# HGRN outputs built token by token on four column tiles, inside the projection's matmuls

## The reference

```python
proj = h @ w_in                                   # q_x, f_x, i_x, g_x, each 8 heads x 128
f = lb + (1.0 - lb) * sigmoid(f_x);  q = silu(q_x);  k = 1.0 - f;  v = i_x
b = cumsum(log(f)) within each chunk of 32
q_rel, k_rel = q * exp(b - b_ref), k * exp(b_ref - b)
a = where(causal, q_rel @ k_rel.T, 0);            o_intra = a @ v
q_dec, k_dec = q * exp(b), k * exp(b_last - b)
# per chunk: o_inter = q_dec @ state;  state = exp(b_last) * state + k_dec.T @ v
o = rms_norm(o_intra + o_inter, o_norm) * silu(g_x)
return o @ w_o
```

## Time and profile before

| | |
|---|---|
| median of 3 runs | 1761.29 us |
| the profiled execution | 1760.62 us, span 1758.8 us, granted clock 0.973 |
| PE busy | 1640.3 us (93%) |
| DVE, ACT, POOL busy | 843.3, 750.8, 649.2 us |
| HGRN heads, loop turns 2 to 7 | some 1129 to 1314 us of the span |

### The profile page before, as it was taken

The page is one execution under the profiler, slowest core; times in us unless marked ns, Lnnn a source line. Parts: engine busy times, 40 slices in busy tenths (PEclk is TensorE's granted clock), DMA queues, the critical chain, the costliest instruction groups (busy, mean ns, idle before and its releaser), DMA issues.

```text
span 1758.8 us, 28713 instructions
## 1 busy us (share of the span) xinstructions
PE 1640.3 (93%) x10394; PEld 1343.9 (76%) x10394; DVE 843.3 (48%) x1461; ACT 750.8 (43%) x1160; POOL 649.2 (37%) x376
## 2 busy tenths in 40 slices
PE   5999979988888999999999999899999999999996
PEld 4787668856566778878888888788878878888885
DVE  6556768856775635522121235566663632111125
ACT  2333334443744445524141347667674622222231
POOL 4453320004421125634444444223334544444441
PEclk9999999989899999999999999899999999999997
DMA  8632210003111112233333331122223233333331
GB/s 288 204 85 72 72 38 3 4 18 87 53 48 34 50 56 78 84 88 92 97 94 97 94 108 48 48 72 72 72 60 92 56 93 96 96 95 95 96 97 59
DMA packets 250958, 140.33 MB, mean 80 GB/s; under 512 B 10121, under 2 KB 242656, under 8 KB 250864
## 3 DMA queue, kind: packets, MB, share of 16 engines
q1 hardware_dynamic: 249552, 137.12, 26.6%
q0 software_dynamic: 1008, 1.66, 0.4%
q10 hardware_dynamic: 304, 0.26, 0.0%
HBM read 136.93 MB, written 2.10 MB: 79 GB/s over the span
## 4 chain that ended last, share of the span: by engine, by line
issue 40%; PE 24%; POOL 11%; DVE 11%; ACT 5%; DVEq 4%; DMA 2%; ACTq 1%; POOLq 1%; SPq 1%
PE bank L750 13%; POOL w_low L555 10%; DVE hg_state L2065 2%; PE bank L1039 2%; DVE bank L2062 2%; PE bank L801 2%; DVEq L2492 1%; DMA x_tok<-in_x 1%; DVE hg_k_dec L2062 1%; PE bank L1199 1%; PE bank L1200 1%; DVEq L2805 1%; PE bank L1227 1%; SPq L439 1%; ACTq L2011 1%
## 5 line engine op out<-in xcount | busy, mean ns | idle before, releaser
L555 POOL TENSOR_TENSOR w_low<-w_raw,w_high 128x1024 fp32r<-128x1024 f32 (+2 forms) x218 | 517.2, 2373 | 964.3 <-ACT w_high L1489 964.2
L750 PE MATMUL bank<-act_high,w_high 128*128 128x512 f32 x976 | 392.4, 402 | 12.1 <-POOL w_low L555 8.4
L750 PE MATMUL bank<-act_high,w_low 128*128 128x512 f32 x976 | 382.7, 392 | 0.0
L750 PE MATMUL bank<-act_low,w_high 128*128 128x512 f32 x976 | 382.6, 392 | 0.0
L1489 ACT ACTIVATE w_high<-w_raw 128x1024 fp32r<-128x1024 f32 (+2 forms) x218 | 219.1, 1006 | 282.2 <-PE bank L750 269.7
L750 PEld LDWEIGHTS bank<-act_high,w_high 128*128 128x128 f32 x976 | 184.4, 189 | 65.3 <-issue 12.3
L750 PEld LDWEIGHTS bank<-act_high,w_low 128*128 128x128 f32 x976 | 184.2, 189 | 40.3
L750 PEld LDWEIGHTS bank<-act_low,w_high 128*128 128x128 f32 x976 | 184.5, 189 | 38.9 <-issue 2.4
L750 PE MATMUL bank<-hid_high,w_high 128*128 128x512 f32 x472 | 184.9, 392 | 3.8 <-DVE mix_out L2734 3.8
L750 PE MATMUL bank<-hid_low,w_high 128*128 128x512 f32 x472 | 184.4, 391 | 0.0
L750 PE MATMUL bank<-hid_high,w_low 128*128 128x512 f32 x472 | 184.3, 390 | 0.0
(11 more groups left out here) (570 smaller groups left out, 2860.0 us busy)
## 6 DMA issues: line engine op xcount, KB each, us to landing
w_raw<-in_mlp_w SPq DMA_DIRECT2D x128, 512.0 KB, 4.0
w_raw<-in_hgrn_w_in SPq DMA_DIRECT2D x32, 512.0 KB, 4.0
w_raw<-in_w_in SPq DMA_DIRECT2D x29, 512.0 KB, 4.0
w_ada_piece<-in_w_ada SPq DMA_DIRECT2D x5, 2048.0 KB, 16.0
w_raw<-in_w_out SPq DMA_DIRECT2D x8, 512.0 KB, 3.8
w_raw<-in_mla_w_o SPq DMA_DIRECT2D x8, 512.0 KB, 3.8
w_raw<-in_hgrn_w_o SPq DMA_DIRECT2D x8, 512.0 KB, 3.8
w_raw<-in_mla_w_in SPq DMA_DIRECT2D x6, 512.0 KB, 4.0
```

The lines of the kernel that those rows point to most:

```text
L555: gp.tensor_tensor(WL[:, c0 % 2, 0:kt, 0:m], WR[:, c0 % 2, 0:kt, 0:m], WH[:, c0 % 2, 0:kt, 0:m].bitcast(F32), ALU.subtract).then_inc(w_lo, 1)
L750: mm = pe.matmul(bank[0:m, :], w[:, k, 0:m], a[:, k0 + k, :], start=(k == 0 and n_ == 0), stop=(k == kt - 1 and n_ == 2))
```

## The change

The outputs become token-major: 32 tokens of the masked scores, or of `hg_q_dec`, are the stationary operand (128x32), the values or the state move (128 columns), and the four chunks of a token tile go to four column tiles of the array. In the loop they are issued inside job 2, after its third slice of K. The root mean square is then a sum along the free axis on VectorE (`tensor_reduce`), the normalisation a multiply from PSUM into a new tile `hg_out_tok`, and four transposes on TensorE bring the result back to feature-major before the last multiply. f is formed by `scalar_tensor_tensor` with the offset broadcast as third operand, and in the loop after the fourth state; k is formed after the states; `low_of_output` goes ahead of job 0's scaling. On ScalarE the gate's SiLU and the squares stand ahead of q's SiLU, the copy of the outputs goes, and a set that holds Ln and Exp is loaded ahead of the exponentials. Some semaphores of the first block are merged (`v_sd` into `u_ready`, `kk_sq` and `rk_ready` into `sums_ready`).

```diff
@@ tensor, hgrn
-                if o is not None:
+                def outputs():
                     for t in range(TT):
-                        pe.matmul(PB[6][:, t * P:(t + 1) * P], VG[:, t, :], AT[:, t, :], start=True, stop=False)
+                        for b in range(P // HC):
+                            pe.matmul(PB[6][b * HC:(b + 1) * HC, t * P:(t + 1) * P], AT[:, t, b * HC:(b + 1) * HC],
+                                      VG[:, t, :], start=True, stop=(t + b == 0))
                         for b in range(P // HC):
                             c_ = t * (P // HC) + b
                             if c_:
                                 pe.wait_ge(g_st, o * (NC - 1) + c_)
-                                mm = pe.matmul(PB[6][:, c_ * HC:(c_ + 1) * HC], ST[:, c_, :],
-                                               QDEC[:, c_ * HC:(c_ + 1) * HC], start=False,
-                                               stop=(b == P // HC - 1))
+                                mm = pe.matmul(PB[6][b * HC:(b + 1) * HC, t * P:(t + 1) * P],
+                                               QDEC[:, c_ * HC:(c_ + 1) * HC], ST[:, c_, :], start=False, stop=True)
                     mm.then_inc(g_out, 1)
...
-                def square_sum():
-                    pe.wait_ge(g_sq, o + 1)
-                    pe.matmul(PB[7][:, :], ONES[:, :], OSQ[:, :], start=True, stop=True).then_inc(g_ss, 1)
...
+                if n is None or second:
+                    outputs()
                 if n is None:
+                    part(W0 + 1, (free["go"], 2), "hgrn_o", 0, 4, HH, HL)
+                elif o is not None and not second:
+                    job(G0 + 2, n * 4, free["g"], n * 4 + 3, amid=outputs)
+                if n is not None and o is not None:
+                    job(G0 + 3, n * 4, free["g"], n * 4 + 4)
+                if o is not None:
+                    pe.wait_ge(g_tok, o + 1)
+                    for t in range(TT):
+                        mm = pe.transpose(PB[6][:, t * P:(t + 1) * P], OTK[:, t, :], IDENT[:, :])
+                    mm.then_inc(g_tr, 1)
+                if n is not None and o is not None:
+                    turn_values(n)
@@ scalar, hgrn (ahead of q's SiLU)
+                if o is not None:
+                    act.wait_ge(free["g"], o * 4 + 6)
+                    act.activation(GG[:, :], TG[3][:, :], ACT.Silu).then_inc(g_gate, 1)
+                    act.wait_ge(g_out, o + 1)
+                    act.activation(OSQ[:, :], PB[6][:, :], ACT.Square).then_inc(g_sq, 1)
...
+                act.preload_act_table_set("natural_log_exp_and_others")
...
-                    act.wait_ge(g_ss, o + 1)
-                    act.activation(OSD[:, :], PB[7][:, :], ACT.Ln, scale=1.0 / P, bias=CST[:, 3:4])
+                    act.wait_ge(g_ms, o + 1)
+                    act.activation(RSQ, MSQ, ACT.Ln, scale=1.0 / P, bias=CST[:, 3:4])
                     act.drain()
-                    act.activation(OSD[:, :], OSD[:, :], ACT.Exp, scale=-0.5).then_inc(g_sd, 1)
-                    act.wait_ge(free["g"], o * 4 + 6)
-                    act.activation(GG[:, :], TG[3][:, :], ACT.Silu).then_inc(g_gate, 1)
+                    act.activation(RSQ, RSQ, ACT.Exp, scale=-0.5).then_inc(g_sd, 1)
@@ vector, hgrn
+                def forget():
                     dve.wait_ge(g_sig, n * 2 + 1)
-                    dve.tensor_scalar(FG[:, :], FG[:, :], LBH[:, 1:2], LBH[:, 0:1], MUL, ADD)
+                    stt(FG[:, :], FG[:, :], LBH[:, 1:2], LBH[:, 0:1].broadcast_to([P, T]), MUL, ADD)
                     after(g_f)
-                    dve.tensor_scalar(KG[:, :], FG[:, :], -1.0, 1.0, MUL, ADD)
...
                     for k in range(T // HC - 1):
+                        if k == 4 and n is not None:
+                            forget()
...
                 if n is not None:
+                    dve.tensor_scalar(KG[:, :], FG[:, :], -1.0, 1.0, MUL, ADD)
                     dve.wait_ge(g_ln, n + 1)
                     dve.tensor_tensor_scan(BG[:, :], HRST[:, :], TG[2][:, :], 0.0, MUL, ADD)
...
                     after(g_diff)
+                if o is not None:
+                    dve.wait_ge(g_sq, o + 1)
+                    dve.tensor_reduce(MSQ, OSQ[:, :].rearrange("p (t d) -> p t d", t=TT), AX, ADD).then_inc(g_ms, 1)
...
                     dve.wait_ge(g_sd, o + 1)
-                    stt(OG[:, :], OG[:, :], col("o_norm"), OSD[:, :], MUL, MUL)
-                    dve.drain()
+                    tt(OTK[:, :, :], PB[6][:, :].rearrange("p (t d) -> p t d", t=TT), bc(RSQ, P), MUL)\
+                        .then_inc(g_tok, 1)
                     dve.wait_ge(g_gate, o + 1)
-                    tt(OG[:, :], OG[:, :], GG[:, :], MUL)
+                    dve.wait_ge(g_tr, o + 1)
+                    stt(OG[:, :], PB[6][:, :], col("o_norm"), GG[:, :], MUL, MUL)
                     after(g_fin)
```

More of the change, by code:

```diff
@@ L194, in block_kernel @@
         OSQ = at("hg_out_sq", 190, [P, T])
-        OSD = at("hg_out_dev", 192, [P, T])
+        OTK = at("hg_out_tok", 192, [P, TT, P])
+        MSQ, RSQ = SMALL[:, 48:48 + TT], SMALL[:, 52:52 + TT]
         VF = at("hg_v_feature", 194, [P, T])
@@ L348, in block_kernel @@
         g_vt, g_vc = sem("g_vt"), sem("g_vc")
-        g_sig, g_gate, g_f, g_ln, g_diff, g_exp, g_ops, g_sc, g_at, g_kt, g_inc, g_st, g_out, g_sq, g_ss, g_sd, g_fin = (
+        g_sig, g_gate, g_f, g_ln, g_diff, g_exp, g_ops, g_sc, g_at, g_kt, g_inc, g_st, g_out, g_sq, g_ms, g_sd, g_fin = (
             sem("g_" + n) for n in ("sig", "gate", "f", "ln", "diff", "exp", "ops", "sc", "at", "kt", "inc", "st", "out",
-                                    "sq", "ss", "sd", "fin"))
+                                    "sq", "ms", "sd", "fin"))
+        g_tok, g_tr = sem("g_tok"), sem("g_tr")
         half_done = sem("half_done")
@@ L1413, in hgrn @@
-                if n is None:
[L1414 to L1422, removed]
+                if n is None or second:
+                    outputs()
+                if n is None:
+                    part(W0 + 1, (free["go"], 2), "hgrn_o", 0, 4, HH, HL)
+                elif o is not None and not second:
+                    job(G0 + 2, n * 4, free["g"], n * 4 + 3, amid=outputs)
@@ L1988, in hgrn @@
                         high(G0 + 3, n * 4)
+                if o is not None:
[3 more added lines that the diff above has]
+                    act.activation(OSQ[:, :], PB[6][:, :], ACT.Square).then_inc(g_sq, 1)
+                if n is not None:
                     act.wait_ge(free["g"], n * 4 + 4)
@@ L1995, in hgrn @@
                     high_spare(W0 + 2)
[L1996 to L2002, removed]
-                    act.sem_inc(g_sq, 1)
+                act.preload_act_table_set("natural_log_exp_and_others")
                 if n is not None:
@@ L2205, in _ @@
                 stt(SQP[:, j, :], R_[:, j, :], col("r_k", j), K_[:, j, :], MUL, MUL)
-            after(rk_ready)
+            after(sums_ready)
             tt(ICL[:, :, :], KKN[:, :, :], ICL[:, :, :], MUL)
@@ L2775, in hgrn @@
                                         HMSK[:, :, :].rearrange("p t s -> p (t s)"), PB[2][:, :]).then_inc(g_at, 1)
+                    if not second:
+                        low_of_output(o - 1)
                 if n is not None:
@@ L2784, in hgrn @@
                     dve.drain()
+                def forget():
                     dve.wait_ge(g_sig, n * 2 + 1)
-                    dve.tensor_scalar(FG[:, :], FG[:, :], LBH[:, 1:2], LBH[:, 0:1], MUL, ADD)
+                    stt(FG[:, :], FG[:, :], LBH[:, 1:2], LBH[:, 0:1].broadcast_to([P, T]), MUL, ADD)
                     after(g_f)
-                    dve.tensor_scalar(KG[:, :], FG[:, :], -1.0, 1.0, MUL, ADD)
+                if n is not None and o is None:
+                    forget()
                 if o is not None:
-                    if not second:
-                        low_of_output(o - 1)
                     dve.wait_ge(g_inc, o + 1)
                     for k in range(T // HC - 1):
+                        if k == 4 and n is not None:
+                            forget()
                         ps = PB[2 + k % (P // HC)][:, k // (P // HC) * P:(k // (P // HC) + 1) * P]
```

21 lines of the change are left out of this document (10 added, 11 removed).

## The result

The changed kernel takes 1778.44 us (median of 4, 1776.46 to 1781.56) against 1762.15 (median of 4, 1759.76 to 1763.86): ratio 1.0085, 95% interval 1.0063 to 1.0107, slower by more than can be mistaken for nothing. The profiled execution is 1778.8 us with a span of 1777.1 and a mean granted clock of 0.962 (before: 1760.62, 1758.8, 0.973). Of the 18.3 us between the spans, 15.95 lie in the six loop turns (184.42 us before, 200.37 after, from scores to scores), 0.2 ahead of them and 2.1 behind the last one's scores, where the granted clock fell once more (from 1392.5 to 1399.3).

What follows compares the result with a forecast made beforehand. It took the chain of waits through VectorE and ScalarE as the bound, PE's own work 0.29 us under it. Chain +3.6 and clock +6.4 gave +10.0 us, 1771 against the median; range 1753 to 1780.

Steps and rivals of the forecast that it cites:

- The chain: Waits through VectorE and ScalarE in one loop turn, ending in PE's transposes; claimed to grow 0.6 us, to 31.1 us.
- the two ends: f after the fourth state: held by GpSimd's remainder, turn 0.6 us longer (the case taken), or not held, 0.15 us longer.
- The term +3.6: Lengthened chain over the six loop turns: 3.6 us more, range 0.9 to 3.6.
- PE's own work: PE's work in a loop turn, claimed to fall from 30.19 to 28.3 us.
- The clock: PE's 2.8 us wait lowers the granted clock, costing 1.52 us in seven of ten loop turns: +6.4 us (0 to 9.1).
- column tiles at 0.058 a pass: Outputs on PE take 3.6 us at the rate of two tiles: 0.7 us more a turn, +4 us.
- Outside the turns: Second call +0.4 us, last call -0.3, merged semaphores nothing: together nothing.
- The first: Rival: chain grows but the clock never falls in the loop; 0.9 to 3.6 us more, 1763; chance 0.20.
- The second: Rival: GpSimd's hold on `hg_k_dec` goes and PE's 28.3 us sets the turn; -13 us, 1748; chance 0.20.
- The third: Rival: the outputs' column tiles don't run side by side, 8.7 us of outputs; 1800 us; chance 0.05.
- The 1.9 us won are lost in both ends: States start 1.9 us earlier, but a hold on f, or on k or the scan, takes it back.
- Two limits on top of each other: In a turn before the change: the chain, 30.48 us, and PE's own work 0.29 us under it.

Runs made afterwards that it cites:

- e1: Changed kernel with three more fp32 matmuls, never read, filling PE's wait for the normalised outputs in the six loop turns; 1766.3 us, ratio 1.0012.
- e9: Changed kernel run once more with no edit; 1778.1 us, ratio 1.0071 to the kernel before.
- e2: Changed kernel with ScalarE's high part put behind the small Ln and Exp and a wait for the four products; 1753.0 us, ratio 0.9927.
- e10: e2 with e7's order, the values' transposes ahead of the wait for the normalised outputs; 1752.9 us, ratio 0.9933 to before.
- e5: Changed kernel with f and k back ahead of the 15 states, f still in three-operand form; 1770.7 us, ratio 1.0028 to before.
- e3: Kernel before with a wait for the four products ahead of ScalarE's high part, left in its place; 1787.9 us, ratio 1.0127.
- e6: Changed kernel with f by the earlier two-scalar form, still between the fourth and fifth state; 1766.7 us, ratio 1.0010 to before.
- e7: Changed kernel with PE's four transposes of the values ahead of the wait for the normalised outputs; 1762.9 us, ratio 0.9983 to before.
- e4: Kernel before without the 15 state matmuls a head of the outputs, their waits kept; 1766.2 us, ratio 1.0003.
- e12: e2 with e5's order on VectorE (f and k ahead of the states) and e7's order on PE; 1746.1 us, ratio 0.9896 to before.
- e8: Kernel before with ScalarE's high part behind the small Ln and Exp and a wait for the four products; 1761.3 us, ratio 0.9981.

## Why the prediction was right, and where it was off

1771 was forecast with 1753 to 1780; 1778.4 came. The sign and the mechanism were right. Point by point:

- **The chain.** Counted from the first state (1230.5 in the prediction, 1207.23 in the trace), the prediction has f's end at 4.2, the scan's at 10.7, the first product at 15.7, the held product's end at 20.4 and the normalising multiply's at 21.9. Measured: 4.22, 10.86, 15.79, 20.46, 21.94. The turn was to be 31.1; e1 shows 31.05. f is held, as chosen of the two ends. The reduce cost nothing, nor did the small Ln and Exp, between which no table load is left. The term +3.6 is measured as 6 x 31.05 - 6 x 30.48 = 3.4.
- **PE's own work.** 28.3 forecast, 31.05 - 3.27 = 27.8 measured: the 62 passes took 2.01 us, 0.032 each, and not 2.4 plus 0.2 for the mode. It is off the path, so the only effect was a wait of 3.27 instead of 2.8, which mattered for the clock.
- **The clock: the term that was mis-sized.** Forecast +6.4 (1.52 in seven of ten turns; 0 to 9.1). Measured in six turns: after's 200.37 - 186.3 = 14.1, less the 1.5 that before pays in its first turn, +12.5. Two things were off. The price was that of the fall behind 1.90 us; behind 3.27 us, from the first transposes (1195.31) to the increments (1206.01, 10.70 us where 7.89 is undisturbed: e1's 0.93 to the scores and 6.96), it is 2.8. And all six turns are disturbed, by 0.5 to 2.9 us, not seven of ten. e9 shows it is no accident of one execution. The 12.5 lie above the term's own upper end of 9.1. The terms' upper ends add up to 12.7, some 1774; that 1778.4 lies within the stated range is owed to the margin above them, of which the prediction explains only 4 us, by column tiles at 0.058 a pass, and those did not come. That part is luck.
- **Outside the turns:** nothing was forecast, +2.3 came, 2.1 of it behind the last scores, beside a clock fall that before's profile doesn't have. Whether the fall makes the 2.1 us wasn't tested.
- **Rivals.** The first (no fall, 1763) is what e1 makes true by force: 1766. The second (hold gone, -13 us) was right about the price: e2 came out 12.7 us under the before run beside it once the hold was taken away, but the change itself does not do that, 2.86 us against 2.88. e2's turn is 29.02 and not 28.3: e10 shows the late remainder ahead of job 0 as the bound. The third is excluded by the 2.01 us.
- **"The 1.9 us won are lost in both ends"** is right for f where it was put; e5 shows 0.58 of it to be had from the old place, with f still in its new form.
- **"Two limits on top of each other"** was one short: e3 found ScalarE's tail as the third.

Sum on the spans: chain 3.4, clock in the turns 12.5, the rest 2.3, together 18.2 of 18.3.

What stays open: what decides, besides its length, whether a wait is followed by a fall, and why e6's median lies so far under e9's with nearly the same wait. Over the six turns the falls cost 14.1 us with waits of 3.27 (after), 9.0 with 3.13 (e6), 9.5 with 2.81 (e5), 3.1 with 2.66 (e7) and 0.2 with 1.10 (e2). Yet single waits of 3.14 (e6) and 2.81 (e5) passed at full clock, and one of 2.41 (e7) did not. The runs show that the length of an undivided wait matters, and that e4's three pieces cost little; no more than that.

## What to carry to other kernels

Before taking work off the engine that the page calls busiest, read one turn of the loop for the chain that ends it: where that chain passes through other engines, the work saved becomes a wait, and a wait in one piece can cost in clock nearly as much as the work saved (12.5 us here, against 2.4 us of PE's work in each of six turns); filling it, splitting it, or taking a held operation off the chain (e12: f first, and the high part behind the products) is what turns the saving into time. Look also at what a shifted operation newly meets: e3 freed one held operation and got another held. A change that is slower may still be the right base: without the hold the old kernel gains some 0.2% (e8), the new one some 1.6% (e2).

## What was not expected of the hardware

- Four fp32 column tiles of 32 ran at 0.032 us a pass (62 in 2.01), faster than the 0.039 of four row tiles in the increments (30 in 1.17).
- PE busy with unread work for 2.6 us more a turn (e1; the wait fell from 3.27 to 0.67) made the kernel 12 us faster.
- A VectorE and a GpSimd operation that start within 0.02 us of each other: in three turns of e3 the VectorE one is held (`hid_low` 2.92 us instead of 0.69), in the other three the GpSimd one is drawn out (2.95 instead of 2.39).
- The pattern of clock falls in the loop repeated in the two profiled executions: the turns of e9 and after agree within 0.03 us though they come from two executions.
